# Attention probabilities transposed as two halves of 64 queries in two row tiles, and sums moved into the banks of the scores, in a two-block transformer kernel

## The reference

```python
def gqa_attend(q, k, v):
    s = jnp.einsum('bkgqd,bksd->bkgqs', qg, k).astype(F32) * (d ** -0.5)
    p = jax.nn.softmax(s, axis=-1).astype(v.dtype)
    return jnp.einsum('bkgqs,bksd->bkgqd', p, v).reshape(b, hq, nq, d)
# diff_attend: softmax(q1 k1) - lam * softmax(q2 k2), then times v
# dilated and neighbourhood attention add a bias and a mask before the softmax
# scan: o_i = q_i S + attn_i (u_i - w_i S);  S = S * g + k_i^T (u_i - w_i S), 8 chunks of 64;
#       o = o * rsqrt(mean(o * o) + eps) * onorm_g * silu(gate)
```

## Time and profile before

| | |
|---|---|
| median of 3 runs | 2518.38 us (2516.83 to 2528.87) |
| the profiled execution | 2523.09 us, span 2521.3 us |
| PE busy | 2459.3 us (98%) |
| DVE, ACT, POOL busy | 1518.0 (60%), 978.4 (39%), 836.6 us (33%) |
| dil / diff pairs | about 86 to 128 / 892 to 974 us of the span |
| na / gqa pairs | about 1093 to 1198 / 1890 to 1977 us |
| scan | about 290 to 330 us |

### The profile page before, as it was taken

One profiled execution on the slowest core, in us unless ns is written; L12 is line 12 of the kernel. 1 busy time (PEld: TensorE's weight loads), 2 busy tenths in 40 slices (PEclk: granted clock), 3 DMA queues, 4 the chain that ended last, 5 costly groups with the idle time before them and its releaser, 6 DMA issues.

```text
span 2521.3 us, 36983 instructions
## 1 busy us (share of the span) xinstructions
PE 2459.3 (98%) x14273; PEld 2002.2 (79%) x14273; DVE 1518.0 (60%) x2135; ACT 978.4 (39%) x1581; POOL 836.6 (33%) x446
## 2 busy tenths in 40 slices
PE   8999999999999999999999999999999999999999
PEld 6678877888886878766888888888887767788887
DVE  6665656458567975686365866644776477524242
ACT  4566643232225464356242122122256432433232
POOL 3433033544441222234222323232323322344443
PEclk9999899999999999999999999999999999999999
DMA  6222023445441101130123434323311121232322
GB/s 244 85 67 76 3 67 117 145 147 176 142 134 34 59 18 41 50 70 2 51 85 123 153 127 131 116 95 97 129 56 49 43 75 42 85 116 92 100 95 89
DMA packets 78679, 228.48 MB, mean 91 GB/s; under 512 B 21568, under 2 KB 23616, under 8 KB 77898
## 3 DMA queue, kind: packets, MB, share of 16 engines
q1 hardware_dynamic: 65176, 177.12, 21.5%
q10 hardware_dynamic: 13362, 49.40, 6.0%
HBM read 224.37 MB, written 2.12 MB: 90 GB/s over the span
## 4 chain that ended last, share of the span: by engine, by line
PE 84%; DVE 7%; issue 4%; ACT 3%; POOL 2%; DMA 0%; SPq 0%; DVEq 0%; POOLq 0%; ACTq 0%
PE ps L272 23%; PE ps L273 22%; PE ps L274 22%; PE ps L853 3%; PE ps L870 2%; PE ps L887 2%; POOL w_lo L2889 1%; DVE rstd L752 1%; PE ps L353 1%; PE ps L355 1%; PE ps L354 1%; PE ps L465 1%; DVE small L952 1%; PE ps L2661 1%; PE ps L883 1%
## 5 line engine op out<-in xcount | busy, mean ns | idle before, releaser
L2889 POOL TENSOR_TENSOR w_lo<-ring,w_hi 128x1024 fp32r<-128x1024 f32 x288 | 703.2, 2442 | 1170.1 <-ACT w_hi L265 666.9
L272 PE MATMUL ps<-act_hi,w_hi 128*128 128x512 f32 x2280 | 841.4, 369 | 3.5 <-POOL w_lo L2889 0.9
L274 PE MATMUL ps<-act_hi,w_lo 128*128 128x512 f32 x2280 | 827.9, 363 | 0.0
L273 PE MATMUL ps<-act_lo_ffn,w_hi 128*128 128x512 f32 (+1 forms) x1408 | 512.9, 364 | 0.0
L272 PEld LDWEIGHTS ps<-act_hi,w_hi 128*128 128x128 f32 x2280 | 428.8, 188 | 92.2 <-issue 15.2
L274 PEld LDWEIGHTS ps<-act_hi,w_lo 128*128 128x128 f32 x2280 | 427.7, 188 | 71.8
L265 ACT CAST w_hi<-ring 128x1024 fp32r<-128x1024 f32 (+1 forms) x167 | 172.6, 1034 | 662.8 <-PE ps L274 610.0
L1268 ACT CAST w_hi<-ring 128x1024 fp32r<-128x1024 f32 (+1 forms) x132 | 137.5, 1043 | 457.6 <-PE ps L274 457.6
L1160 DVE SCALAR_TENSOR_TENSOR ada_place<-ada_place 128x1024 f32<-128x1024 f32 x180 | 285.2, 1585 | 24.3 <-DMA ada_place<-in_w_ada 10.0
L273 PEld LDWEIGHTS ps<-act_lo_ffn,w_hi 128*128 128x128 f32 x1408 | 265.1, 188 | 41.1
L272 PE MATMUL ps<-hidden_hi,w_hi 128*128 128x512 f32 x704 | 256.5, 364 | 1.8 <-DVE hidden_lo L1351 1.5
(11 more groups left out here) (422 smaller groups left out, 3383.3 us busy)
## 6 DMA issues: line engine op xcount, KB each, us to landing
ring<-in_w_ffn SPq DMA_DIRECT2D x204, 512.0 KB, 3.3
ada_place<-in_w_ada ACTq DMA_DIRECT2D x90, 512.0 KB, 4.2
ring<-in_w_gdn SPq DMA_DIRECT2D x16, 512.0 KB, 3.3
ring<-in_w_hy SPq DMA_DIRECT2D x12, 512.0 KB, 3.3
ring<-in_w_dil_qk SPq DMA_DIRECT2D x8, 512.0 KB, 8.8
ring<-in_w_out SPq DMA_DIRECT2D x8, 512.0 KB, 3.2
ring<-in_w_diff_qk SPq DMA_DIRECT2D x8, 512.0 KB, 3.3
ring<-in_w_na_qk SPq DMA_DIRECT2D x8, 512.0 KB, 3.3
```

What stands on the lines that cost most here:

```text
L272: pe.matmul(out, w[0], x[0], start=start, stop=False)
L273: pe.matmul(out, w[0], x[1], start=False, stop=False)
L274: return pe.matmul(out, w[1], x[0], start=False, stop=stop)
L2889: pool.tensor_tensor(k.w_lo[:, a % SPLITS, :], k.ring[:, a % SLOTS, :], k.w_hi[:, a % SPLITS, :].bitcast(F32), ALU.subtract).then_inc(k.lo ...
```

## The change

Blocks of probabilities are transposed as two halves of 64 queries, in two row tiles, one half into bank 6 and one into bank 7, up to 8 blocks in a phase; one copy takes a phase (or each engine a half of it, in dil). A wide pair that is not joined has two phases, opening and closing, any other one. Sums go to the empty half of bank 2 or 5 of their pair's scores, so scores and sums now wait for each other. The orders of PE, DVE and ACT in an iteration are new. The lines' matmuls stand behind tile 4 of the projection, in banks 1 and 3, and their copy and transfer follow there. In the scan the squares are taken once for two steps over all 128 partitions, the scaling follows the copies, the transposes stand at n = 4, 6 and behind the last step, and the gating goes by halves of 256 columns. The diff, cut to its core:

```diff
-        if j == 3 and stored is not None:
+        if j == 1 and stored is not None:
             pe.wait_ge(*stored)
...
+                    if i == 1 and stored is not None:
+                        pe.wait_ge(*stored)
...
-                elif stored is not None:
-                    pe.wait_ge(*stored)
...
+TURNED = 8
+Phase = collections.namedtuple("Phase", "a b ways turned kept copies")
...
+    def __init__(self, k, pairs, third, before, opened, wide=(0, 0, 0), by=("act", "act")):
...
-        self.chunks, self.use, self.freed = {}, {}, []
-        for p in range(N + 1):
-            if p < N:
-                it = pairs[p]
-                total, self.chunks[p] = it["blocks"] * (1 if it["joined"] else 2), []
-                for c, a in enumerate(range(0, total, 4)):
-                    by = "dve" if c == 1 and not it["joined"] else "act"
-                    count["chunks"], count[by] = count["chunks"] + 1, count[by] + 1
-                    self.chunks[p].append((by, len(self.freed), a, min(a + 4, total), count["chunks"], count[by]))
-                    self.freed.append((self.copied[by], count[by]))
-            if p >= 1:
-                self.use[p - 1] = len(self.freed)
-                self.freed.append((self.stored, self.nth(p)))
+        self.phases, kept = {}, (self.first["act"], self.first["dve"])
+        for p, it in enumerate(pairs):
+            n = it["blocks"]
+            spans = [(0, 0, n)] if it["joined"] else [(1, 0, 2 * n)] if 2 * n <= TURNED else [(0, 0, n), (1, n, 2 * n)]
+            self.phases[p] = []
+            for which, a, b in spans:
+                ways = [(by[which], 0, 2)] if by[which] != "both" else [("act", 0, 1), ("dve", 1, 2)]
+                count["phases"] += 1
+                for engine, _, _ in ways:
+                    count[engine] += 1
+                self.phases[p].append(Phase(a, b, ways, count["phases"], kept, (count["act"], count["dve"])))
...
+    def opening(self, p):
+
+        return self.phases[p][:1] if 0 <= p < len(self.pairs) and len(self.phases[p]) == 2 else []
+
+    def closing(self, p):
+        return self.phases[p][-1:] if 0 <= p < len(self.pairs) else []
...
-    def turn_bank(self, use):
-        return 6 + use % 2
-
-    def reuse(self, pe, use):
-
-        if use >= 2:
-            pe.wait_ge(*self.freed[use - 2])
+    def sum_column(self, p):
+
+        return 512 * (3 * (p % 2) + 2)
+
+    def copies_ready(self, pe, copies):
+        pe.wait_ge(self.copied["act"], copies[0])
+        if copies[1] > 0:
+            pe.wait_ge(self.copied["dve"], copies[1])
...
+            if a == CTX and n > S and p >= 4:
+                pe.wait_ge(*self.stored_to(p - 3))
...
-    def turn(self, pe, p, first, end):
-        k, it = self.k, self.pairs[p]
-        if first == 0:
-            self.open(pe, "turn", p)
-        for _, use, a, b, _, _ in self.chunks[p][first:end]:
+    def turn(self, pe, p, phases):
+
+        k = self.k
...
+            if ph.a == 0:
...
             if it["joined"]:
                 pe.wait_ge(self.mixed, self.first["mixed"] + self.joined[p] + 1)
             else:
-                pe.wait_ge(self.scaled, self.first["scaled"] + 2 * p - self.joined[p] + 1 + (b > it["blocks"]))
-            self.reuse(pe, use)
-            for i in range(a, b):
+                pe.wait_ge(self.scaled, self.first["scaled"] + 2 * p - self.joined[p] + 1 + (ph.b > it["blocks"]))
+            if ph.kept[0] > 0:
+                self.copies_ready(pe, ph.kept)
+            for i in range(ph.a, ph.b):
                 g = i + it["blocks"] if it["joined"] else i
-                last = pe.transpose(k.bank(self.turn_bank(use), P, (i - a) * P), self.sets[p % 3][:, g * P:(g + 1) * P],
-                                    k.const("ident"))
+                for h in range(2):
+                    r = slice(HD * h, HD * h + HD)
+                    last = pe.transpose(k.bank(6 + h, HD, (i - ph.a) * HD), self.sets[p % 3][r, g * P:(g + 1) * P],
+                                        k.const("ident")[r, r])
             last.then_inc(self.turned, 1)
...
     def sum(self, pe, p):
-        k, it, use = self.k, self.pairs[p], self.use[p]
+        k, it = self.k, self.pairs[p]
         self.open(pe, "sum", p)
-        for by, _, _, _, _, copies in self.chunks[p]:
-            pe.wait_ge(self.copied[by], copies)
-        self.reuse(pe, use)
-        out, n = self.turn_bank(use) * 512, it["blocks"]
+        self.copies_ready(pe, self.phases[p][-1].copies)
+        if p + 2 < len(self.pairs):
+            if self.pairs[p + 2]["bias"] is None:
+                pe.wait_ge(self.exps, 2 * self.nth(p + 3))
+            else:
+                pe.wait_ge(self.maxed, 2 * self.nth(p + 3))
+        if p >= 2:
+            pe.wait_ge(*self.stored_to(p - 1))
+        out, n = self.sum_column(p), it["blocks"]
...
     def tensor(self, pe, begun=0):
         N = len(self.pairs)
         for p in range(N + 4):
-            first = 1 if self.pairs[0]["joined"] else 2
-            if 3 <= p < N + 3:
-                self.turn(pe, p - 3, 0, first)
+            if p >= 4:
+                self.sum(pe, p - 4)
+            self.turn(pe, p - 3, self.closing(p - 3))
             if begun <= p < N:
                 self.score(pe, p)
             if p < 3:
                 wide_products(self.k, pe, self.fill[p])
-            if 3 <= p < N + 3:
-                self.turn(pe, p - 3, first, 3)
-            if p >= 4:
-                self.sum(pe, p - 4)
+            self.turn(pe, p - 2, self.opening(p - 2))
+
+    def copy(self, e, engine, copying, p, phases):
+
+        for ph in phases:
+            for by, first, end in ph.ways:
+                if by == engine:
+                    e.wait_ge(self.turned, ph.turned)
+                    src = self.k.bank(6, 2 * 512).rearrange("p (h g c) -> p h g c", h=2, c=HD)[:, first:end, 0:ph.b - ph.a, :]
+                    dst = self.probs_turned(p, ph.a, ph.b).rearrange("p (g h c) -> p h g c", h=2, c=HD)[:, first:end, :, :]
+                    copying(dst, src).then_inc(self.copied[engine], 1)
...
-        def copy(p, first, end):
-            for by, use, a, b, turned, _ in self.chunks[p][first:end]:
-                if by == "act":
-                    s.eng.wait_ge(self.turned, turned)
-                    s.eng.copy(self.probs_turned(p, a, b), k.bank(self.turn_bank(use), (b - a) * P)).then_inc(self.copied[by], 1)
...
+                s.eng.wait_ge(self.turned, self.phases[p - 3][-1].turned)
...
-            if p >= 3:
-                copy(p - 3, 0, 1)
+            self.copy(s.eng, "act", s.eng.copy, p - 3, self.opening(p - 3))
             if p <= N:
                 exp(p - 1, 0)
+            self.copy(s.eng, "act", s.eng.copy, p - 3, self.closing(p - 3))
+            if p <= N:
                 exp(p - 1, 1)
-            if p >= 3:
-                copy(p - 3, 1, 3)
...
+            if p >= 2 and not (h == 1 and self.pairs[p - 2]["joined"]):
+                v.eng.wait_ge(self.scaled, self.first["scaled"] + 2 * (p - 2) - self.joined[p - 2] + 1 + h)
...
             v.eng.wait_ge(self.summed, self.nth(p + 1))
-            v.eng.tensor_copy(self.pairs[p]["out"], k.bank(self.turn_bank(self.use[p]), P)).then_inc(self.stored, 1)
-
-        for p in range(N + 4):
-            if 3 <= p < N + 3:
-                for by, use, a, b, turned, _ in self.chunks[p - 3]:
-                    if by == "dve":
-                        v.eng.wait_ge(self.turned, turned)
-                        v.eng.tensor_copy(self.probs_turned(p - 3, a, b), k.bank(self.turn_bank(use), (b - a) * P))\
-                            .then_inc(self.copied[by], 1)
+            v.eng.tensor_copy(self.pairs[p]["out"], k.ps[:, self.sum_column(p):self.sum_column(p) + P])\
+                .then_inc(self.stored, 1)
+
+        for p in range(N + 3):
+            self.copy(v.eng, "dve", v.eng.tensor_copy, p - 3, self.closing(p - 3))
             if p < N:
                 v.eng.wait_ge(self.scores, self.nth(p) + 1)
                 largest(p, 0)
-            if 1 <= p <= N:
-                invert(p - 1, 0)
-            joined = self.pairs[0]["joined"]
-            if p >= 4 and not joined:
-                store(p - 4)
-            if p < N:
-                largest(p, 1)
-            if p >= 4 and joined:
-                store(p - 4)
             if 1 <= p <= N:
                 invert(p - 1, 1)
                 if self.pairs[p - 1]["joined"]:
@@ -991,6 +1004,12 @@
                     v.eng.wait_ge(self.scaled, self.first["scaled"] + 2 * (p - 1) - self.joined[p - 1] + 1)
                     v.eng.scalar_tensor_tensor(self.probs(p - 1, 1), self.probs(p - 1, 1), self.small(p - 1, 8, 1),
                                                self.probs(p - 1, 0), ALU.mult, ALU.add).then_inc(self.mixed, 1)
+            if p < N:
+                largest(p, 1)
+            if p >= 3:
+                store(p - 3)
+            if p < N:
+                invert(p, 0)
```

(89 more changed lines are left out.)

24 lines of the change are left out of this document (11 added, 13 removed).

## The result

The changed kernel takes 2541.66 us (median, 2538.13 to 2543.51, 6 runs) against 2521.61 before beside it: ratio 1.0081, 95% interval 1.0064 to 1.0098, so 20 us slower where I forecast 15.5 us faster, and outside my range of 2484 to 2520. The profiled execution's span is 2541.7 us (before: 2521.3).

What follows compares the result with a forecast made beforehand. PE was taken to bound it, with 84% of the chain of waits. Lines -1.0, dil -4.5, na -14, gqa -11, diff +23 and scan -8 summed to -15.5: 2507.6 us like the profiled execution, median 2503, range 2484 to 2520.

Steps and rivals of the forecast that it cites:

- Diff, +23 forecast: In diff, a closed loop of waits takes wide pairs from 3.23 to a mean of 4.63 us; +23 (0 to +30).
- loop M: In diff: largest(p, 1), exp, copy of 768, exp, reciprocal, mixed, next largest; 4.98 us a wide pair.
- short pairs unchanged: In diff, only the 16 wide pairs were counted as slower; short pairs were to keep their time.
- loop S: Named in follow-ups, in diff: last scores, two maxima, reciprocal and mixed, store and signal, next scores; 4.57 us a wide pair.
- three full cycles -10: In na, six pairs take 22.2 us in place of 25.56; three cycles give -10, the end -4, together -14.
- 11 to 12: In gqa's end, 15.6 us from last scores to next product become 11 to 12, -4 of the stage's -11.
- I take 0.9 per cycle: In dil, a four-pair cycle gains 0.9 us, four cycles, and 1 for the stage's end; -4.5 (0 to -7).
- Half transposes: In attention, a block as two 64-column records in two row tiles takes PE 0.06 us, between bounds 0.055 and 0.109.
- Rival E: Half transposes cost a full slot, so only the changes of tile shape are saved; 2511 us, chance 0.13.
- Scan, -8 forecast: Scan: 2.0 us from n = 2 and 6, 6 from the clock staying up; -8 (-2 to -9).
- C: Scan's clock still falls, giving 2 not 8; half of na's and gqa's gain lost to store waits; 2514 us, chance 0.15.
- D: PE's clock falls in diff and PE enters the loop; +31, 2534 us, chance 0.10.

Runs made afterwards that it cites:

- mixed late: Changed kernel, but in diff DVE takes the second reciprocal and mixed(p-1) behind largest(p, 1) again; 2529.4 us, 1.0034 of before.
- the fastest kernel here: Changed kernel with before's attention class for dil and diff, the new one for na and gqa, new scan and lines; 2502.1 us, 0.9924 of before.

## Why the prediction was wrong

Between the forecast of -15.5 and the +20.4 of the table lie 35.9 us: diff 10.4, dil 6.8, na 6.8, gqa 5.4, and 6.5 of dense stretches for which the sum had no term. So not one step failed but one in each attention stage's term, all to the same side.

- **Diff, +23 forecast, +33.4 measured.** The loop M I had added up, 4.98, is in the profile to the hundredth, where the copy in it is a wide pair's:

```profile
954.99 0.95 DVE L978 TENSOR_REDUCE small<-ps 128x1 f32<-128x768 f32 x1
...
957.37 0.96 DVE L978 TENSOR_REDUCE small<-ps 128x1 f32<-128x768 f32 x1 [0.15 <-PE ps L867]
...
959.97 0.95 DVE L978 TENSOR_REDUCE small<-ps 128x1 f32<-128x768 f32 x1
```

  From one second maximum to the next it is 959.97 - 954.99. The four wide pairs of this cycle take 4.74 + 4.57 + 4.58 + 4.98 = 18.9. That the forecast had 18.6 is partly luck: it had 4.0, 4.6, 4.98 and 4.98, but the first waited 1.5 for its scores and took 4.74, and the third took 4.58, since the copy in its loop is still a short pair's. The two short ones take 5.32 + 3.12 = 8.4. The step that failed is "short pairs unchanged" at 2 x 3.2: the first short pair still stands behind a wide one's exps, copy and mixed, 4.98, plus clock. That is 2 us in each cycle; the stage's start (5.7, with 10 us of low clock) and end (2.9) are the rest. And loop S, 4.57, which I had used for na ("score's last columns now wait for stored(p-4)"), I did not look for in diff, where it bounds two of the four wide pairs and lies just below M for the others. So I would have named the wrong cure: mixed moved alone gave diff 6.4 us back, the store moved as well 25.7 (with the copy).
- **na, -14 forecast, -7.2 measured.** A cycle came out as forecast, 22.2 against 22.40. The step that failed is "three full cycles -10": I had multiplied before's slowest cycle. By its stores the three took 25.55, 24.10 and 23.31 us, so they gained 3.15, 1.69 and 0.90. The end, for which I had counted -4, gave 1.7: from the last pair's first scores to the next dense product it went from 15.5 to 13.9, and the last store stands 2.94 behind the one before it, earlier 1.31. The clock took a part: 6.8 us at 1.2 GHz in this stage, none before; executions of the same na code without it stand at -8.6.
- **gqa, -11 forecast, -5.6 measured.** A pair takes 4.06, 3.96 was forecast; whether the loop that I added up bounds it or PE, busy for 31.18 of 32.49 us, no run parts. The step that failed is the end, "11 to 12" for the stretch from the last scores to the next product: it went from 15.6 to 14.6, -1 and not -4. Most of the rest is at the start, where 13.7 us were at 1.2 GHz (10.2 before); with 3.4 there, in the kernel with dil and diff old, gqa stands at -7.8 with the same end. PE and DVE in the changed kernel, then PE before:

```profile
1985.40 0.59 PE L889 MATMUL ps<-consts,pair_probs 64*128 64x64 f32 x12
...
1991.08 0.59 PE L889 MATMUL ps<-consts,probs 64*128 64x64 f32 x12 [1.15 <-DVE pair_turned L935]
...
1994.74 1.53 PE L911 MATMUL ps<-pair_turned,big 128*64 128x128 f32 x24 [1.10 <-issue]
```

```profile
1989.97 0.96 DVE L935 COPY pair_turned<-ps 128x768 f32<-128x768 f32 x1 [0.22 <-PE ps L889]
```

```profile
1970.40 0.63 PE L870 MATMUL ps<-consts,big 128*128 128x128 f32 x4 [0.33 <-ACT pair_turned L913]
...
1974.47 2.84 PE L887 MATMUL ps<-pair_turned,big 128*64 128x128 f32 x48
```

  A phase fills both banks 6 and 7, so the next one waits for its whole copy (0.96). Chunks of four had two banks in turn: before, the last stores came 3.74, 3.51 and 1.31 behind each other, now 3.94, 3.71 and 3.14. PE's waits in the stretch add up to 3.9 us (1.7 of them for POOL), before to 1.1. My step "sums go ahead of turns there, banks 6 and 7 are free of sums" saw the banks' new freedom and not that two buffers had become one. This is read from the waits; no run has the new order with two buffers.
- **dil, -4.5 forecast, +2.3 measured.** The same waits for copies stand at the end, PE's timeline:

```profile
124.34 0.66 PE L911 MATMUL ps<-pair_turned,big 128*64 128x128 f32 x8 [1.52 <-DVE pair_turned L935]
...
126.22 1.35 PE L911 MATMUL ps<-pair_turned,big 128*64 128x128 f32 x12 [0.70 <-ACT pair_turned L935]
...
129.45 1.97 PE L911 MATMUL ps<-pair_turned,big 128*64 128x128 f32 x16 [0.83 <-ACT pair_turned L935]
```

  The last pair's store comes 3.85 behind the one before it, earlier 0.87. A part of this is clock: it is at 1.2 GHz from 126.5 to 133.3, and with whole transposes, where it isn't, the interval is 2.95. The step that failed in the steady part is "I take 0.9 per cycle": eight pairs take 19.05 us where the clock stays up (mixed late), 18.95 before. PE is busy for 15.95 us of the window in place of 17.66, but its sums wait 2.9 for DVE's copies, a wait that before did not have.
- **Half transposes**, 0.06 a block: right. The twelve records at 1985.40 are six pairs of halves, 0.059 apart but for the first. Rival E did not hold for them. "TensorE: Matmul & The Clock Gate", section LDWEIGHTS, in the Trainium skill gives columns divided by 1.2 as the ns of a load, 107 for 128 columns whatever the rows; each half loads 128 columns, and the pairs do not stand that far apart.
- **Scan, -8 forecast**: -8.1 between the products, the clock at 1.00 throughout; -4 in the medians. **Lines**, -1.0: -0.85, the idle time gone.
- **The rivals.** No rival had the mechanism. C spoke of "waits of scores for stores", but in na and gqa and as 5 us. D named the clock in diff, 31 us for it; that its 2534 lies nearest to the result is luck: the low clock came, in short stretches, and was worth a few us. My sum had no term for a clock that moves.

## What to carry to other kernels

Before buffers are merged, write down for each wait the closed loop that it makes, with every instruction queued between its two ends, in each stage by itself: the longest sets the time and the next one shows up as soon as that is cut. A store of 0.28 us that frees a bank belongs right behind its data and ahead of long work, but not ahead of work that its own data waits for. A steady cycle says nothing of the stage's start and end, nor is one cycle as long as the next: count them by themselves. At the end waits show, here those for the one buffer's copy, that the cycle had hidden.

## What the runs showed of the hardware

Repeated runs of one kernel spread with the mean granted clock: 21 runs of before lie between 2515.2 and 2524.6 us, 1.85 us for each 0.001 of clock, correlation -0.95; the changed kernel's runs lie at 0.985 to 0.989, the mean of those 21 is 0.995. Stretches at 1.2 GHz, 3.4 to 13.7 us long but for one at the very end, add up to 41 us in before's profiled execution, 79 in the changed kernel's, 10 in that of the fastest kernel here. A forecast to a few microseconds needs a term for it, and a difference of a few needs many runs.
